# Four weight buffers for the down products of both feed-forwards, and two moves at the start of each, in a float32 encoder step on one core

## What is computed

```python
def swiglu(x, w_in, w_out):
    gate, up = jnp.split(x @ w_in, 2, axis=-1)
    return (jax.nn.silu(gate) * up) @ w_out

h = swiglu(rmsnorm(x, g[0]), lw['ffn_in'][0], lw['ffn_out'][0])
x = x + FFN_RES * rmsnorm(h, g[1])          # D_FF = 2816 = 22 tiles of 128, FFN_RES = 0.5
```

## Time and profile before

| | us |
|---|---|
| median of 3 runs | 2779.25 |
| lowest, highest | 2779.01, 2781.45 |
| profiled execution, its own time | 2778.04 |
| its span, first to last instruction | 2776.2 |
| busy: PE, its weight loads, DVE, ACT, POOL | 2630.7, 2509.6, 1701.9, 1134.6, 415.1 |
| mean granted clock of TensorE, share of full | 0.983 |

### The profile page before, as it was taken

The page is one execution under the profiler, slowest core; times in us unless marked ns, Lnnn a source line. Parts: engine busy times, 40 slices in busy tenths (PEclk is TensorE's granted clock), DMA queues, the critical chain, the costliest instruction groups (busy, mean ns, idle before and its releaser), DMA issues.

```text
span 2776.2 us, 46136 instructions
## 1 busy us (share of the span) xinstructions
PE 2630.7 (95%) x17839; PEld 2509.6 (90%) x17839; DVE 1701.9 (61%) x2685; ACT 1134.6 (41%) x1901; POOL 415.1 (15%) x346
## 2 busy tenths in 40 slices
PE   7999999999999899999999999989989998999998
PEld 7999999897679899999888999989966898999998
DVE  5566574647666666647476574755575747657474
ACT  4243343425544434334343342443164534334243
POOL 0010111102244001011100110120022330011011
PEclk9999999999999999999999999999999999999998
DMA  3223232320015132322203232243101160323222
GB/s 106 73 68 99 61 97 75 94 56 11 23 46 94 38 84 57 99 72 82 85 27 95 61 97 79 69 109 80 26 10 33 38 107 27 95 61 97 84 64 82
DMA packets 370019, 191.54 MB, mean 69 GB/s; under 512 B 38525, under 2 KB 365520, under 8 KB 369870
## 3 DMA queue, kind: packets, MB, share of 16 engines
q1 hardware_dynamic: 365870, 179.08, 24.2%
q0 software_dynamic: 4000, 10.47, 1.7%
HBM read 183.58 MB, written 5.93 MB: 68 GB/s over the span
## 4 chain that ended last, share of the span: by engine, by line
PE 85%; DVE 8%; ACT 4%; issue 2%; DMA 1%; DVEq 0%; SPq 0%; ACTq 0%
PE ps L674 24%; PE ps L675 24%; PE ps L676 24%; PE ps L1014 2%; DVE w L2046 1%; PE ps L1023 1%; ACT w L1442 1%; DVE y L2176 1%; PE ps L1142 1%; DMA raw<-in_w_ffn_in_dram 1%; PE ps L1074 1%; DVE w L2030 1%; PE ps L1056 1%; DVE at L2457 1%; PE ps L1120 1%
## 5 line engine op out<-in xcount | busy, mean ns | idle before, releaser
L674 PE MATMUL ps<-xh,w 128*128 128x320 f32 x2304 | 725.6, 315 | 47.6 <-DVE ub L2163 16.1
L675 PE MATMUL ps<-xl,w 128*128 128x320 f32 x2304 | 718.9, 312 | 0.0
L676 PE MATMUL ps<-xh,w 128*128 128x320 f32 x2304 | 718.5, 312 | 0.0
L1442 ACT ACTIVATE w<-raw 128x512 fp32r<-128x512 f32 (+3 forms) x393 | 348.9, 891 | 533.9 <-PE ps L676 513.2
L674 PEld LDWEIGHTS ps<-xh,w 128*128 128x128 f32 x2304 | 439.0, 191 | 59.3 <-DVE xl L2236 21.2
L674 PE MATMUL ps<-hh,w 128*128 128x320 f32 x1408 | 445.7, 317 | 38.8 <-DVE w L2046 38.8
L675 PE MATMUL ps<-hl,w 128*128 128x320 f32 x1408 | 441.4, 314 | 0.0
L676 PE MATMUL ps<-hh,w 128*128 128x320 f32 x1408 | 441.3, 313 | 0.0
L675 PEld LDWEIGHTS ps<-xl,w 128*128 128x128 f32 x2304 | 439.1, 191 | 0.3
L676 PEld LDWEIGHTS ps<-xh,w 128*128 128x128 f32 x2304 | 438.8, 190 | 0.0
L2817 POOL TENSOR_TENSOR hl<-ub,hh 128x640 fp32r<-128x640 f32 x88 | 174.1, 1979 | 1568.7 <-ACT hh L1442 1465.0
(11 more groups left out here) (400 smaller groups left out, 4057.9 us busy)
## 6 DMA issues: line engine op xcount, KB each, us to landing
raw<-in_w_ffn_in_dram SPq DMA_DIRECT2D x178, 512.0 KB
raw<-in_w_ffn_out_dram SPq DMA_DIRECT2D x192, 192.0 KB
raw<-in_w_in_dram SPq DMA_DIRECT2D x38, 512.0 KB
raw<-in_w_ffn_out_dram SPq DMA_DIRECT2D x64, 128.0 KB
raw<-in_w_out_dram SPq DMA_DIRECT2D x12, 512.0 KB
out_dram<-xio SPq DMA_DIRECT2D x5, 512.0 KB
xin<-in_x_prompt_dram SPq DMA_DIRECT2D x1, 2048.0 KB, 8.0
y<-in_cache_ckv_dram POOLq DMA_DIRECT2D x8, 256.0 KB, 3.3
```

The costliest lines, as they stand in the source:

```text
L674: pe.matmul(out, wh, xh, start=first, stop=False, skip_group_check=loose)
L675: pe.matmul(out, wh, xl, start=False, stop=False, skip_group_check=loose)
L676: return pe.matmul(out, wl, xh, start=False, stop=last, skip_group_check=loose)
L1442: return nc.scalar.activation(out, in_, func, **kw)
```

## The change

- Down units use four buffers instead of two, unit k in buffer k mod 4: in RAW 1024 columns each, in W 1536 columns each for high and low. Each buffer has a semaphore for its loads (`arrived` replaces `turn`).
- SP loads d0 as before, d1, d2 and d3 as soon as the low part of the last up unit is done, and dk for k of 4 and more when that of d(k-4) is.
- ACT and DVE split d0 to d3 during or just behind the last up unit, and d(k+4) when dk is done. In ACT's queue of the last down stage the split now stands ahead of the square.
- The first splits of the next part's first Strassen unit follow d4, d5 and d7 (`FIRST_FREED`); its four block sums, and in the first part `fourth_lo`, stand on DVE between the emptying of d4 and of d5.
- The down loops are written out on PE, ACT, DVE and SP.
- At the start of a feed-forward ACT scales X (`g_of_x`) ahead of the end of the third unit's split and of R.
- DVE copies the first up product out of PSUM to UB without waiting for silu, which frees the banks, and multiplies it from there (`gated`).

```diff
+DEEP = 4
+def buffer_of(n):
+    for base in (FFN0, FFN1):
+        for p, tiles in enumerate(PARTS):
+            k = n - (base + PART_AT[p] + tiles)
+            if 0 <= k < DOWN:
+                return k % DEEP
+    return n % 2
+LOADED_BY = [buffer_of(n) for n in range(UNITS)]
+LOADS = [LOADED_BY.count(b) for b in range(DEEP)]
...
-FREED_BY = (0, 2, 4, 5)
+FREED_BY, FIRST_FREED = (0, 2, 4, 5), (4, 5, 7, 7, 7)
...
-    loaded = [sem("loaded0"), sem("loaded1")]
+    loaded = [sem(f"loaded{b}") for b in range(DEEP)]
...
+    def arrived(l, n, i=0):
+        l, n = l + n // UNITS, n % UNITS
+        b = LOADED_BY[n]
+        return loaded[b], (l * LOADS[b] + LOADED_BY[:n + 1].count(b) + i) * LOAD_INC
...
-    def down_w(j, n):
-        at = j * 4096
+    def down_raw(k, n):
+        at = 1024 * (k % DEEP)
+        return RAWF[:, at:at + n * P]
+    def down_w(k, n):
+        at = 2 * HMAX * P * (k % DEEP)
...
# SP
-        def load(u, j, pieces, hold=False):
-            sp.wait_ge(lo_ready, u + 1)
+        def load(u, b, pieces, hold=False, behind=2):
+            sp.wait_ge(lo_ready, u - behind + 3)
...
-            with sp.Fori(0, DOWN // 2) as i:
+            for k in range(DOWN):
+                dst = down_raw(k, n).rearrange("p (k n) -> p k n", n=P)
+                load(unit(l, base, 0, k), k % DEEP,
...
+                     behind=(2, 2, 3)[k] if k < 3 else DEEP)
...
# ACT
+        def split_third_hi_end(l, base):
             cut = slice(READ * 256, KD * 256)
...
-        def split_hi_d(l, base, i, j, n):
-            act.wait_ge(loaded[j % 2], turn(l, base + j - j % 2, i, 0))
-            act.wait_ge(unit_done, unit(l, base, i, j) + 1)
+        def split_hi_d(l, base, k, n, freed):
+            act.wait_ge(*arrived(l, base + k))
+            act.wait_ge(*freed)
...
# ACT, strassen_up, last unit of a part
-                    split_hi_d(l, at + n, 0, 1, n)
+                    split_hi_d(l, at + n, 1, n, pd_ps.nth(l, LASTP * g + 2))
+                    split_hi_d(l, at + n, 2, n, pd_ps.nth(l, LASTP * g + 4))
+                    split_hi_d(l, at + n, 3, n, pd_ps.nth(l, LASTP * g + 5))
...
# ACT, plain_up
                 if k == 3:
-                    split_hi_d(l, base + n, 0, 0, n)
+                    for i in range(DEEP):
+                        split_hi_d(l, base + n, i, n, (unit_done, u + 2 + i // 2))
...
+        def down(l, base, n, stage=None, after=None):
+            for k in range(DOWN - 1):
+                u = unit(l, base, 0, k)
+                if k < DOWN - DEEP:
+                    split_hi_d(l, base, k + DEEP, n, (unit_done, u + 3))
+                if stage is not None:
+                    square_y(l, k, u, stage)
+                elif k >= DOWN - DEEP:
+                    after(k)
...
         def ffn(l, f, base):
             split_third_hi(l, base, 2 * f)
-            inverse_rms_x(l, 2 * f)
...
             g_of_x(l, f)
+            split_third_hi_end(l, base)
+            inverse_rms_x(l, 2 * f)
             plain_up(l, f, base)
...
# DVE, plain_up
                 if k == 3:
-                    split_lo_d(l, base + n, 0, 0, n)
+                    split_lo_d(l, base + n, 0, n)
+                    split_lo_d(l, base + n, 1, n)
                 dve.wait_ge(unit_done, u + 3)
+                if k == 0:
+                    dve.wait_ge(*r_ready.nth(l, 6 * f))
+                V.tensor_tensor(*gate, two(R[:, :]), ALU.mult).then_inc(gate_ready.sem, 1)
+                if k == 3:
+                    split_lo_d(l, base + n, 2, n)
+                    split_lo_d(l, base + n, 3, n)
+                if k == 0:
+                    dve.wait_ge(*hl_ready.nth(l, h0 - 2))
+                    V.tensor_copy(*up).then_inc(drained, 1)
+                    dve.wait_ge(drained, u + 3)
+                    gated(l, j, h0)
+                    continue
...
# DVE, down
+            for k in range(DOWN - 1):
+                evicted(k)
+                if k < DOWN - DEEP:
+                    split_lo_d(l, base, k + DEEP, n)
+                elif stage is None:
+                    after(k)
```

More of the change, by code:

```diff
@@ L554, in down @@
             src = A["w_ffn_out"][l, f].rearrange("(k p) n -> p k n", p=P)
-            with sp.Fori(0, DOWN // 2) as i:
[L556 to L561, removed]
+            for k in range(DOWN):
+                dst = down_raw(k, n).rearrange("p (k n) -> p k n", n=P)
+                load(unit(l, base, 0, k), k % DEEP,
+                     [(dst[:, h * n // 2:(h + 1) * n // 2, :],
+                       src[:, first + h * n // 2:first + (h + 1) * n // 2, k * P:(k + 1) * P]) for h in range(2)],
+                     behind=(2, 2, 3)[k] if k < 3 else DEEP)
         def ffn(l, f, base):
@@ L1525, in finish, with square_y, silu @@
             tile_of_x(3)
-        def square_y(l, i, j, u, stage):
+        def square_y(l, k, u, stage):
             act.wait_ge(drained, u + 3)
[L1529 to L1533, removed]
+            act.wait_ge(*sq_added.nth(l, ADD * stage + k - 1))
+            run(GB[:, k % 2, :], Y[:, k, :], ACT.Square).then_inc(sq_ready.sem, 1)
+        def silu(l, j, h, done):
+            act.wait_ge(*done)
             run(GB[:, j, :], GB[:, j, :], ACT.Silu).then_inc(silu_ready.sem, 1)
@@ L1551, in group_hi @@
             if q == 0:
[L1552 removed]
+                act.wait_ge(unit_done, unit(l, at, 0, 0) + FIRST_FREED[n] - 5)
             elif n == G_S4:
@@ L1573, in strassen_up @@
             for q in range(n):
-                j, g = q % 2, strassen(f, p, q)
+                j, g, u = q % 2, strassen(f, p, q), unit(l, at, 0, q)
                 more = q + 1 < n
@@ L1628, in fourth_hi @@
             run(XH[:, 0:QUARTERS, N2], T4[:, :, :], ACT.Copy).then_inc(xc_act.sem, 1)
-        def down(l, base, n, stage=None):
-            with act.Fori(0, DOWN // 2 - 1) as i:
-                for j in range(2):
-                    if stage is not None:
-                        square_y(l, i, j, unit(l, base, i, j), stage)
-                    split_hi_d(l, base, i, j + 2, n)
-            if stage is not None:
-                i = DOWN // 2 - 1
-                square_y(l, i, 0, unit(l, base, i, 0), stage)
-                split_hi(l, base, i, 2)
+        def down(l, base, n, stage=None, after=None):
+            for k in range(DOWN - 1):
+                u = unit(l, base, 0, k)
+                if k < DOWN - DEEP:
[4 more added lines that the diff above has]
+                    after(k)
+            if stage is None:
+                after(DOWN - 1)
+            else:
+                split_hi(l, base, 0, DOWN)
         def ffn(l, f, base):
             split_third_hi(l, base, 2 * f)
-            inverse_rms_x(l, 2 * f)
             if f:
@@ L1653, in ffn, with first_splits @@
                 if p + 1 < len(PARTS):
-                    down(l, at + n, n)
-                    if p == 0:
-                        fourth_hi(l, f, base)
-                    for s in range(len(GROUPS)):
-                        group_hi(l, base + PART_AT[p + 1], 0, strassen(f, p + 1, 0), s)
+                    def first_splits(k):
+                        if p == 0 and k == FIRST_FREED[0]:
+                            fourth_hi(l, f, base)
+                        for s, freed in enumerate(FIRST_FREED):
+                            if freed == k:
+                                group_hi(l, base + PART_AT[p + 1], 0, strassen(f, p + 1, 0), s)
+                    down(l, at + n, n, None, first_splits)
                 else:
@@ L2153, in plain_up @@
                 j, u = k % 2, unit(l, base, 0, k)
+                up = two(UB[:, j, :]), PS[:, 4 * j + 2:4 * j + 4, 0:HALF]
+                gate = two(GB[:, j, :]), PS[:, 4 * j:4 * j + 2, 0:HALF]
                 if k == 2:
```

138 lines of the change are left out of this document (61 added, 77 removed).

## The result

| | before | after |
|---|---|---|
| median of four runs each, side by side, us | 2780.11 | 2687.07 |
| lowest, highest | 2779.01, 2781.45 | 2683.46, 2687.92 |
| span of the profiled execution | 2776.2 | 2681.7 |
| busy: PE, DVE, ACT, POOL | 2630.7, 1701.9, 1134.6, 415.1 | 2598.0, 1681.1, 1131.6, 418.0 |
| mean granted clock | 0.983 | 0.995 |

The changed kernel takes 0.9665 of the time before, with a 95% interval of 0.9653 to 0.9678, so it is 93 us faster. The forecast was 2686, in a range of 2677 to 2702. PE is busy for 33 us less although it runs the same matmuls. Nearly all of that is the clock.

A forecast was written before the change was run, and what follows sets the result against it. PE's stalls and slow clock in the feed-forwards were taken as the bound, 101.8 us; 8.4 would stay, so 93.4 off the profiled 2778.04 gives 2684.6, plus 1.2 for the median, said as 2686; range 2677 to 2702.

The forecast's parts named there:

- The bound: Feed-forwards: PE's stalls and slow clock cost 101.8 us, some 25.5 each, all that the change can reach there.
- (a): Third up unit: 4.0 us stall and slow clock go, 6.9 us; new 0.2 us stall at the fourth up unit.
- The sum: Left per feed-forward 2.1 us, four times 8.4; saved 93.4 of 101.8, giving a median of 2686 us.
- (b): First part's d1: of a 2.9 us stall 0.3 (0 to 0.6) is left, the last H tile being late.
- (c): d2 in each of four parts: 0.4 us stays for emptying d0's PSUM, 1.6 per feed-forward; ends 0 and 0.6.
- (d): First Strassen unit behind the first part: 2.4 us stall goes; 6.3 us fits before d7 at 6.7, at worst 0.5.
- (e): Written-out loops, SP's moved loads, squares behind the split: nothing; six loads in a row after the last up unit stay hidden.
- Nothing left (1): Feed-forwards: the stalls leave nothing at all, 2677.5 us; chance 0.08 for under 2681.
- Thin places that break (2): Fourth up unit, `fourth_lo` and sums, d2 or clock overrun by 1.5 to 4 us a feed-forward: 2692 to 2702; chance 0.20.
- Late loads (3): Loads land late, ACT blocks silu, last tile late in 16 places: up to 2752 us; chance 0.04 for 2702 to 2774.
- Instruction fetch (4): Written-out down stages make PE stand at each new 256 instructions, 14 places: slower than before, over 6.6 us each; chance 0.02.

The follow-up runs named there:

- copy_no_move: Changed kernel with the scaling of X put back behind R, the up product's copy kept: 2708.13 us, ratio 0.9744 to the kernel before.
- move_no_copy: Changed kernel without the copy of the first up product, the scaling of X still ahead of R: 2690.82 us, ratio 0.9681 to the kernel before.
- two_orders: Changed kernel, d0 finished earlier before d1 in six-tile parts; first part's d2, d3 splits behind silu (ACT) and up product (DVE): 2684.52 us, ratio 0.9663.
- late_loads: Changed kernel, but SP loads each down unit when the low part of the unit two before is done: 2689.73 us, ratio 0.968.
- after_again: The changed kernel run once more, nothing edited: 2687.58 us beside 2778.7 of the kernel before, ratio 0.9676.
- loops_rest: Kernel before with the down loops of ACT, DVE and SP written out, PE's kept: 2775.89 us, ratio 0.9987.

## Why the prediction was right, point by point

- **The bound.** PE's stalls and its slow clock were the whole of what could be had: 101.8 us were counted as missing, 4 x 2.35 = 9.4 are still missing. Predicted to be left: 8.4.
- **(a)** Right in what happens: the stall of 4.0 us and the slow clock behind it are gone, ACT's scalings hidden, the table loaded ahead of the wait. The new wait at the fourth up unit was put at 0.2; the pitch of 0.27 and the one after it add up to 0.23 more than natural. `copy_no_move` and `move_no_copy` showed that the order of ACT, not PSUM, was the heart of it. Its price of 6.9 us was read from one stall and is the upper end of 5.4 to 6.9; undoing both moves cost 5 to 5.6 a feed-forward, where 6.9 less the new 0.2 would be 6.7. The sum does not use this price: it starts from the 101.8 us counted as missing, in which the cheaper stall of the second feed-forward (158 matmuls missing there, 178 and 179 in the others) is contained.
- **(b)** Inside its bounds (0.3 predicted, 0 to 0.6; a pitch of 0.61 - 0.15 = 0.46 measured, and 0.07 in the next one), wrong in place, so that the size is in part luck. I had looked at the last H tile only: with POOL at 84.70 to 86.28 it is ready before PE asks at 83.89 + 18 x 0.147 = 86.5. What PE waits for is the bank of the last up unit, at the start of d1. The step that failed is the one that followed the two splits from the up product to H but not to `drained`, though the same product frees both; `two_orders` took it away.
- **(c)** Right: 0.4 predicted, four times in a feed-forward. Measured 0.44 - 0.15 = 0.29 and 0.07 in the next pitch, each time: 0.36, or 1.4 in all for the 1.6.
- **(d)** Right: no wait. From the start of d4's emptying at 99.48 to the end of d5's at 105.71 it took 6.23 us for the predicted 6.3. PE begins d7, which needs that PSUM, at 106.33, 0.6 behind it and without a pause; of this 0.15 is the hand-over, so 0.5 was to spare where 0.4 was predicted. DVE, then PE:

```profile
99.48 0.82 DVE L2225 COPY y<-ps 128x640 f32<-128x640 f32 x1 [2.10 <-PE ps L702]
...
104.89 0.82 DVE L2225 COPY y<-ps 128x640 f32<-128x640 f32 x1
...
106.33 0.31 PE L700 MATMUL ps<-hh,w 128*128 128x320 f32 x1
```

- **(e)** The loops were put at nothing in the sum, and in the changed kernel that holds, since the stalls they lengthened are gone. In the kernel before they cost some 7 us, which the prediction did not know; these were inside the 101.8 us. The six loads in a row stayed hidden, and `late_loads` shows that sending them early matters little.
- **The sum.** Predicted saving 93.4 in one execution, found 94.5 between the spans: 92.4 in the feed-forwards, and 2 outside of them that no step of the sum has. The steps left in each feed-forward add up to 0.23 + 0.53 + 1.4 + 0 = 2.2 for the predicted 2.1 and the counted 2.35. That the median came within some 1 us of the forecast is luck all the same: the four runs of the changed kernel lie between 2683.46 and 2687.92, and the profiled one is the fastest of them.
- **The rivals.** Nothing left (1): no, 9.4 us are. Thin places that break (2): the narrow ones held; the fourth unit's weights came as late as foreseen, and d7 had some 0.5 us to spare. Late loads (3): not in the changed kernel; in `late_loads` the mechanism exists, covered in the six-tile part that was looked at and with a cost of 1.05 us in one of the four first parts. Instruction fetch (4): the written-out loops were faster, not slower.

## What to carry over

Before a buffer is added, write down for each engine's queue what the moved work now stands in front of, and follow every semaphore that the delayed instruction counts up; one instruction may free a bank and feed a product at once. When an engine's in-order list makes another wait, removing the wait's immediate cause (here PSUM, by a copy) shifts the stall to the next customer of the same list: move the work in the list first. A stall costs more than its length where it pulls the clock down, and counting matmuls in a window against a clean window gives the whole price, which the list of waits doesn't.

## What the hardware showed that I had not expected

- **The same wait, another clock.** Waits of PE of 4.02 us had a granted clock of 0.77 or 0.89 over 15 us, one or the other within a single execution. The wait of 2.84 gave 0.89 in the first feed-forward of `copy_no_move` and 0.77 in the second (60.00:75.00 and 945.82:960.82); the waits of 1.1 us inside a feed-forward left it at 1.00.
- **A start inside a loop body.** ACT's square came 0.17 to 0.18 us later behind DVE's emptying than in straight code. What PE's waits gained by it was 0.3 us at four places, not 0.17 at each of twenty.
- **Slow clock that comes and goes, and here cost nothing.** At the seam ahead of the second feed-forward PE has nearly the same waits in every kernel here, the longest 1.68 us. The changed kernel's window at 896.00, above, has 0.83. The same stretch before, then in `after_again`, the same kernel as the changed one, and last `after_again` at the seam ahead of the fourth feed-forward:

```profile
919.74:929.74 10.00, 6.96 (x43) 1.00 0.24 68
```

```profile
896.03:906.03 10.00, 6.96 (x43) 1.00 0.24 70
2219.83:2229.83 10.00, 8.21 (x43) 0.83 0.24 70
```

So this is no effect of the change: two executions of one kernel have it at different seams. All these windows hold 43 matmuls, at 0.83 as at 1.00, because PE waits there for DVE anyway and the slow matmuls fill the wait: the next wait, for a low part, is 0.24 us long in the changed kernel and 1.05 in `after_again`, and ends at 902.27 and 902.29. It is not always free: the window of `loops_rest` at this seam (921.30:931.30) has 0.66 and 32 matmuls. What decides where the clock falls was not found.
